# Cached values of four sequences at once, each in 32 columns of its own, in five steps between attention and output units

## What is computed

```
for g, (window, dil) in enumerate(((128, 1), (512, 4), (2048, 16))):     # 3 head groups x 4 heads of 64
    idx = L + arange(4)[:, None] - dil * arange(window // dil + 1)[None, :]
    s = einsum('bshd,bsjhd->bshj', q, ext_k[:, idx]) * 64 ** -0.5
    p = softmax(s); o = einsum('bshj,bsjhd->bshd', p, ext_v[:, idx])
o_att = sum over g of softmax_g(log-sum-exp) * o                          # then @ w_att, gates, @ w_out, FFN
```

## Time and profile before

| | |
|---|---|
| median of 3 runs | 1829.3 us |
| the profiled execution | 1829.45 us, span 1827.7 us |
| PE busy | 1750.7 us (96%), 10,208 matmul passes |
| DVE, ScalarE, GpSimd busy | 1047.1, 458.5, 74.1 us |
| granted TensorE clock, mean | 0.981 of full speed |
| share of PE in the chain that ended last | 83% |
| the 144 passes of the cached values | 899.4 to 944.8 us |

### The profile page before, as it was taken

One profiled execution on the slowest core, in us unless ns is written; L12 is line 12 of the kernel. 1 busy time (PEld: TensorE's weight loads), 2 busy tenths in 40 slices (PEclk: granted clock), 3 DMA queues, 4 the chain that ended last, 5 costly groups with the idle time before them and its releaser, 6 DMA issues.

```text
span 1827.7 us, 24930 instructions
## 1 busy us (share of the span) xinstructions
PE 1750.7 (96%) x10208; PEld 1623.5 (89%) x10208; DVE 1047.1 (57%) x1471; ACT 458.5 (25%) x900; POOL 74.1 (4%) x133
## 2 busy tenths in 40 slices
PE   5999989999998998999889999999999999999999
PEld 5899989999998888998657799899899899899897
DVE  5688998788987576586614532442433433433425
ACT  5111122323443464612202322111111111111120
POOL 0000000000000011120210000000000000000000
PEclk8999999999999999999999999999999999999999
DMA  6111243334333347984562022122222222222232
GB/s 194 52 56 58 75 134 117 104 98 165 104 111 105 136 130 223 300 278 151 190 224 75 1 81 93 63 91 89 92 92 92 92 93 92 92 92 93 92 107 100
DMA packets 156485, 211.53 MB, mean 116 GB/s; under 512 B 9090, under 2 KB 127010, under 8 KB 155603
## 3 DMA queue, kind: packets, MB, share of 16 engines
q1 hardware_dynamic: 145971, 134.01, 23.7%
q0 software_dynamic: 10416, 76.16, 11.2%
HBM read 180.04 MB, written 74.80 MB: 139 GB/s over the span
## 4 chain that ended last, share of the span: by engine, by line
PE 83%; DVE 7%; DMA 3%; DVEq 2%; SPq 1%; issue 1%; ACT 1%; ACTq 0%; POOL 0%; POOLq 0%
PE ps L723 19%; PE ps L724 19%; PE ps L725 19%; PE ps L1167 4%; PE ps L1165 4%; PE ps L1166 4%; DVE conv L1528 2%; PE ps L1091 2%; PE ps L1093 2%; PE ps L1092 2%; PE ps L937 1%; DMA qb<-scr_q 1%; SPq L489 1%; PE ps L811 1%; PE ps L990 1%
## 5 line engine op out<-in xcount | busy, mean ns | idle before, releaser
L723 PE MATMUL ps<-xhi,whi 128*128 128x352 f32 x1200 | 407.0, 339 | 8.8 <-DVEq L1584 7.3
L725 PE MATMUL ps<-xhi,wlo 128*128 128x352 f32 x1200 | 389.0, 324 | 0.0
L724 PE MATMUL ps<-xlo,whi 128*128 128x352 f32 x1200 | 388.8, 324 | 0.0
L723 PE MATMUL ps<-nhi,whi 128*128 128x352 f32 x1056 | 340.8, 323 | 0.8 <-DVE nlo L1890 0.8
L724 PE MATMUL ps<-nlo,whi 128*128 128x352 f32 x1056 | 338.5, 321 | 0.0
L725 PE MATMUL ps<-nhi,wlo 128*128 128x352 f32 x1056 | 338.2, 320 | 0.0
L1528 DVE SCALAR_TENSOR_TENSOR conv<-u,vec,conv 128x1024 f32<-128x1024 f32 x240 | 308.3, 1285 | 25.2 <-issue 10.6
L1484 DVE TENSOR_TENSOR wlo<-raw,whi 128x1024 fp32r<-128x1024 f32 x126 | 153.6, 1220 | 247.2 <-ACT whi L1255 239.0
L723 PEld LDWEIGHTS ps<-xhi,whi 128*128 128x128 f32 x1200 | 229.0, 191 | 19.6 <-DVEq L1584 7.8
L724 PEld LDWEIGHTS ps<-xlo,whi 128*128 128x128 f32 x1200 | 229.5, 191 | 4.4 <-issue 0.2
L725 PEld LDWEIGHTS ps<-xhi,wlo 128*128 128x128 f32 x1200 | 228.7, 191 | 0.0
(11 more groups left out here) (224 smaller groups left out, 2002.2 us busy)
## 6 DMA issues: line engine op xcount, KB each, us to landing
kv_sample<-cache_kv_w POOLq DMA_DIRECT2D x32, 1022.0 KB, 6.3
raw<-w_in SPq DMA_DIRECT2D x50, 512.0 KB, 4.6
raw<-w_gate_up SPq DMA_DIRECT2D x44, 512.0 KB, 3.9
scr_z<-zt SPq DMA_DIRECT2D x34, 528.0 KB, 3.2
qb<-scr_q POOLq DMA_DIRECT2D x24, 512.0 KB, 5.6
raw<-w_down SPq DMA_DIRECT2D x22, 512.0 KB, 4.2
kc<-cache_kv_w POOLq DMA_DIRECT2D x16, 512.0 KB, 6.7
vc<-cache_kv_w POOLq DMA_DIRECT2D x16, 512.0 KB, 6.0
```

The source lines that it names most:

```text
L723: pe_mm(out, wh, rhs_hi, start=first, stop=False)
L724: pe_mm(out, wh, rhs_lo, start=False, stop=False)
L725: return pe_mm(out, wl, rhs_hi, start=False, stop=last)
```

## The change

The eight sequences are taken as even ones (par 0) and odd ones (par 1). A step takes one group and one parity, four sequences x = 0..3, each with its own 32 columns of the array and its own 32 PSUM rows, and the inner loop goes over x: four matmuls in a row that share no column. Group 0 is one step with both parities. The five steps stand behind units 10 (att 10), 15 (att 15), 16, 17 and 18 (out 0, 1, 2). UNITS is shifted by one: out 0 to 3 stand before att 16. Nine buffers of a tile each are used: v5, v6, v7, v1, v2 on x1's tiles, raw0 and raw1 (the weight staging buffers), va0 and va1 (the old vc3, vc4). Group 0's tiles come four sequences per DMA. In spread_probs a semaphore stands in place of the drain. The residual tiles 1 and 2 are now loaded when steps 1 and 2 are done, 3 to 7 when step 4 is done, and the first FFN weight tile, which lay in raw0 from before att 0, is loaded after them.

```diff
-    vc = [at(f"vc{i}", [P, DEC_S, GW], F32, S3 + (KT - 3 + i) * D * 4) for i in range(3)]
-    vc += [at(f"vc{3 + i}", [P, DEC_S, GW], F32, S4 + i * D * 4) for i in range(2)]
+    v5, v6, v7, v1, v2 = (at(f"vc{t}", [P, DEC_S, GW], F32, S3 + t * D * 4) for t in (5, 6, 7, 1, 2))
+    vr = [raw[(ATT0 + i) % 2][:, :].rearrange("p (s d) -> p s d", s=DEC_S) for i in range(2)]
+    va = [at(f"va{i}", [P, DEC_S, GW], F32, S4 + i * D * 4) for i in range(2)]
+    VBUF = [[v5, v6], [v7, v1, vr[0], vr[1]], [v2, v5, v6, va[0]], [v7, vr[0], vr[1], va[1]], [v5, v6, va[0], v7]]
...
-    VTILES = [0] * 16 + [12, 12]
+    VSTEPS = [(0, 0), (1, 0), (2, 0), (1, 1), (2, 1)]
+    VSTEP_AT = {10: 0, 15: 1, 16: 2, 17: 3, 18: 4}
+    V_END = 18
...
-        for t in range(KT - 5):
+        residual_load(0)
+        att_gate_load(2)
+        for t in range(1, 3):
+            sp.wait_ge(s_kcf, t + 1)
             residual_load(t)
-        att_gate_load(2)
-        sp.wait_ge(s_pv, 1)
-        for t in range(KT - 5, KT):
+        sp.wait_ge(s_kcf, len(VSTEPS))
+        residual_load(3)
+        residual_load(4)
+        wo_load(1, 0, 2)
+        for t in range(5, KT):
             residual_load(t)
-        wo_load(1, 0, 2)
+        ffn_load(FFN0)
...
-            nc.gpsimd.memset(ptz[:, :, :, :], 0.0)
-            nc.gpsimd.memset(ptz0[:, :, :], 0.0)
+            nc.gpsimd.memset(ptz[:, :, :, :], 0.0).then_inc(s_pz, 1)
+            nc.gpsimd.memset(ptz0[:, :, :], 0.0).then_inc(s_pz, 1)
             pool.wait_ge(s_ptr, 1)
-            pool.drain()
+            pool.wait_ge(s_pz, 2)
...
-            dst = ps[32 * (b // 2):32 * (b // 2) + 32, 7, 0:GW]
-            for s in range(DEC_S if g else 1):
-                w = ptz[:, g - 1, DEC_S * b + s, :] if g else ptz0[:, b, :]
-                mm = nc.tensor.matmul(dst, w, vc[n % 5][:, s if g else DEC_S - 1, :], start=b % 2 == 0 and g == 0,
-                                      stop=b % 2 == 1 and g == NG - 1 and s == DEC_S - 1, skip_group_check=True)
+            pe.wait_ge(s_vc[n], 16 * len(VBUF[n]))
+            for s in range(DEC_S if g else 2):
+                for x in range(DEC_B // 2):
+                    if g:
+                        w, v = ptz[:, g - 1, DEC_S * (2 * x + par) + s, :], VBUF[n][x][:, s, :]
+                    else:
+                        w, v = ptz0[:, 2 * x + s, :], VBUF[0][s][:, x, :]
+                    mm = nc.tensor.matmul(ps[32 * x:32 * x + 32, 7, 0:GW], w, v, start=n == 0 and s == 0,
+                                          stop=n == len(VSTEPS) - 1 and s == DEC_S - 1, skip_group_check=True)
```

More of the change, by code:

```diff
@@ L346, in build @@
     TAP0 = KT * TAPS_GLU + 6 * NG * TAPS_QKV
[L348 to L351, removed]
-    VTILES = [0] * 16 + [12, 12]
-    V_END = len(VTILES) - 1
-    assert sum(VTILES) == NB and UNITS[V_END] == ("out", 1)
+    UNITS = [("att", c * KT + j) for c in range(2) for j in range(KT)] + [("out", t) for t in range(4)]
+    UNITS += [("att", 2 * KT + j) for j in range(4)] + [("out", 4)] + [("att", 2 * KT + j) for j in range(4, KT)]
+    UNITS += [("out", o) for o in range(5, DNG)]
+    N_EARLY = UNITS.index(("out", 5))
+    VSTEPS = [(0, 0), (1, 0), (2, 0), (1, 1), (2, 1)]
+    VSTEP_AT = {10: 0, 15: 1, 16: 2, 17: 3, 18: 4}
+    V_END = 18
+    assert UNITS[V_END] == ("out", 2)
     w_in = a["w_in"][0]
@@ L588, in _ @@
                     block_store(n)
-                if q % NCH == 1:
+                if q % NCH == 1 and GATE0 + jj + 3 < FFN0:
                     job_load(GATE0 + jj + 3)
@@ L656, in _, with value_heads, value_tile @@
             cache_copy(1, b)
+        def value_heads(par):
+            c = a[caches[0]][0, par:DEC_B:2, :, 1].rearrange("b t h d -> t b (h d)")
+            pool.dma_start(VBUF[0][par][:, :, :], c).then_inc(s_vc[0], 16)
+        def value_tile(n, x):
+            g, par = VSTEPS[n]
+            c = a[caches[g]][0, 2 * x + par, :, 1].rearrange("t h d -> t (h d)")
+            pool.dma_start(VBUF[n][x][:, :, :], c.rearrange("(i r) d -> i r d", r=DIL[g])[:, 0:DEC_S, :]).then_inc(s_vc[n], 16)
         def cache_tile(tile, sem_, kind, g, b):
@@ L695, in _ @@
         pool.wait_ge(s_g, NSLOT)
[L696 to L705, removed]
+        value_heads(0)
+        value_heads(1)
+        value_tile(1, 0)
+        value_tile(1, 1)
+        spread_probs()
+        pool.wait_ge(s_lo, ATT0 + 1)
+        value_tile(1, 2)
+        pool.wait_ge(s_lo, ATT0 + 2)
+        value_tile(1, 3)
+        value_tile(2, 0)
+        pool.wait_ge(s_kcf, 1)
+        value_tile(2, 1)
+        value_tile(2, 2)
+        pool.wait_ge(s_hlo, 2 * KT)
+        value_tile(2, 3)
+        value_tile(3, 3)
+        pool.wait_ge(s_kcf, 2)
+        for x in range(3):
+            value_tile(3, x)
+        pool.wait_ge(s_kcf, 3)
+        for x in range(3):
+            value_tile(4, x)
+        pool.wait_ge(s_kcf, 4)
+        value_tile(4, 3)
         for b in range(DEC_B):
@@ L980, in cache_values @@
         def cache_values(n):
-            g, b = n % NG, n // NG
+            g, par = VSTEPS[n]
             if n == 0:
-                pe.wait_ge(s_pz, 1)
+                pe.wait_ge(s_pz, 3)
                 pe.wait_ge(s_oTl, 5)
-            pe.wait_ge(s_vc[n % 5], 16 * (n // 5 + 1))
-            dst = ps[32 * (b // 2):32 * (b // 2) + 32, 7, 0:GW]
-            for s in range(DEC_S if g else 1):
-                w = ptz[:, g - 1, DEC_S * b + s, :] if g else ptz0[:, b, :]
-                mm = nc.tensor.matmul(dst, w, vc[n % 5][:, s if g else DEC_S - 1, :], start=b % 2 == 0 and g == 0,
-                                      stop=b % 2 == 1 and g == NG - 1 and s == DEC_S - 1, skip_group_check=True)
+            pe.wait_ge(s_vc[n], 16 * len(VBUF[n]))
[7 more added lines that the diff above has]
+                                          stop=n == len(VSTEPS) - 1 and s == DEC_S - 1, skip_group_check=True)
             mm.then_inc(s_kcf, 1)
@@ L1113, in _ @@
                 out_unit(r, i)
[L1114 to L1118, removed]
+            if r in VSTEP_AT:
+                cache_values(VSTEP_AT[r])
+            if r == V_END:
+                new_values()
             if kind == "out":
@@ L1911, in _ @@
         split_lo(1, FFN0 + 1, 0)
-        for t in range(4, NT):
+        for t in range(5, NT):
             residual(0, t)
-            if t >= 5:
-                wo_lo(1, t - 5)
+            wo_lo(1, t - 5)
         for t in range(NT + 2):
```

## The result

The changed kernel takes 1813.63 us (median of 4 runs, 1807.61 to 1814.55) against 1830.87 of the kernel before on the same chip: ratio 0.9912, 95% interval 0.9891 to 0.9932. A second set of runs gave 0.9901 (0.9885 to 0.9916). So the gain is 16 to 18 us, where 24.7 were forecast (ratio 0.987).

What follows compares the result with a forecast made beforehand. PE bounds the kernel, busy 96% of the span. The 24.7 us gain is 22.3 overlap, 1.0 step 0 now covered and 1.4 waits and clock: 1829.45 - 24.7 = 1804.8 us, range 1799 to 1814.

Steps and rivals of the forecast that it cites:

- the overlap: Value steps on PE: four column blocks run at once, 18 rounds in 8.8 us against 31.1, a gain of 22.3 us.
- the rate at which passes are handed to PE: Possible limit in the value steps: 0.061 us a pass, so 0.49 us a round rather than 0.43.
- C: Rival for the value steps: no overlap, 6.9 us a step, gain 11.2 us, 1818.2 us; chance 0.11.
- B: Rival for the value steps: two matmuls at a time, a round 0.86 us, gain 19.9 us, 1809.5 us; chance 0.14.
- what sets step 2: Ahead of step 2, PE idles from 901.0 to 907.2 for va0's load, issued only after att 15's low half is written.
- Steps 1, 3 and 4: Value steps whose tiles land in time; each should wait less than 1 us.
- The drain: GpSimd idled 9.02 us there; whether its replacement frees GpSimd earlier is swallowed by the wait ahead of step 2.
- the slow clock: Behind the wait ahead of step 2: 3 us of work at half rate, so step 2 takes 3.3 us instead of 1.96.
- the gate chunk: Load beside the value tiles: ends about 1 us later, near 887.5, inside the slack before DVE needs it at 890.06.
- the step on what is behind: Units after new_values: same work in the same dependence, residual tile 3 and the first FFN weight tile in time, nothing lost.
- part 3: Forecast's last part: the 24.7 us gained by 926.7, where out 2 is done, carries whole to the end, giving 1804.8 us.

Runs made afterwards that it cites:

- e_one_block: Changed kernel with all four sequences of a step on the first column block and first 32 PSUM rows, part of the result not computed; ratio 0.9981 to the kernel before.
- e_seq_outer: Changed kernel with the two inner loops swapped, all tokens of one sequence before the next sequence; ratio 0.9955 to the kernel before.
- e_out4_last: Changed kernel with att 16 to 23 in one piece behind out 3, so out 4 stands between att 23 and out 5; ratio 0.9894 to the kernel before.
- e_before_out4: Kernel before with out 4 moved from behind att 23 to behind out 3, so out 5 stands next to att 23; ratio 1.0041.
- e_no_release: Changed kernel with out 4 behind att 23 and buffers dealt so no step waits for the one just before it; 1800.53 us, ratio 0.9834 to the kernel before.
- e_no_release_wo: e_no_release with DVE writing each low part of the second half's output weights one out unit earlier; 1793.57 us, ratio 0.9806 to the kernel before.
- e_late_gate: Changed kernel, out 4 behind att 23, step 2's last tile in residual tile 0's place, third gate chunk loaded after step 3; ratio 0.9869 to the kernel before.
- e_drain: Changed kernel with the GpSimd drain back in place of the semaphore wait for the two memsets; ratio 0.9887 to the kernel before.
- e_v0: Changed kernel with step 2's last tile in residual tile 0's place instead of va0, residual tile 0 loaded after step 2; ratio 0.9885 to the kernel before.

## Why the prediction came out as it did

**Right: the overlap.** The prediction took full overlap of four column blocks from a glimpse of two. Measured are 1.86 us a step at full clock (1.73 would be 4 times 0.43, I took 1.96), so the rate at which passes are handed to PE is at most a small part of it. C (no overlap) is what e_one_block measures, 7.0 us a step, and the changed kernel is far from it. B fails too: a step would have taken 3.5 us.

The Trainium skill ("TensorE: Matmul & The Clock Gate", Part 3, what overlaps and what doesn't) has matmuls starting and ending in program order. The runs don't agree: a step whose passes come in pairs per block took 1.86 us, and in e_seq_outer a pass of the second sequence started at 924.54, before three of the first that precede it in the order. The same Part 3 of the Trainium skill (the mechanism, drawn for tiles in different rows) gives tiles side by side the time of one and about 4 ns for each further one. Here, for four column blocks, a round took 1.86 / 4 = 0.465 us against 0.43 for one matmul, so it is close to that but somewhat more.

**Right: what sets step 2.** PE waited 6.05 us there (6.2 forecast), for va0's load behind att 15's low half, which landed in 4.01 us (4.12 forecast). Steps 1, 3 and 4 waited for nothing. The drain made no measurable difference.

**Slightly off: the slow clock and the gate chunk.** The granted clock was 0.51 from 908.8 to 915.6, so that step 2 and the start of out 1, 5.2 us of work from 910.4 on, ran at the lower level, and not 3 us: step 2 took 3.6 us rather than 3.3, and out 1 6.4 rather than 5.75. The second gate chunk took 14.2 us to land, not some 11, and was there at 893.4, so it delayed DVE's att 8 and with it att 15's low half: the load that waits for that half was issued 27.5 us behind the first value load, against 26.9 before. Together out 3 began 930.6 - 878.9 = 51.7 us behind the first value load, where 926.7 - 876.1 = 50.6 were forecast: 1.1 us.

**Wrong: the step on what is behind.** "The rest of the list is the same work in the same dependence" was false. Out t of the first half needs chunk 2 as soon as its tokens reach beyond 704, that is from t = 5 on. Before the change out 4 stood between att 23 and out 5, and its 5.6 us covered the time in which DVE caught up with the four att units ahead of it (about 1.56 us each against PE's 0.95). The change spent that cover: with UNITS shifted by one, out 3 went ahead of att 16 and out 4 between att 19 and att 20, and nothing was left between att 23 and out 5. I counted the units and not what each may wait for. It cost 3.85 us of waiting and 18.3 - 16.7 = 1.6 of slow clock. e_out4_last takes 5.2 to 5.5 us away by undoing just this (4.7 of it in the stretch up to out 5, where 0.7 us of the wait stay), and e_before_out4 makes the wait appear in the kernel before, at 5.6 us in the same stretch. So the term of the sum that failed is part 3's, the gain at out 2 carried whole to the end: 24.7 us forecast there, of which this step lost 5.5.

24.7 less 1.1 less 5.5 is 18.1, and the remainder gained 17.8. That the measured 1813.6 us still lies in the range from 1799 to 1814 is luck: its upper part was drawn for B, which the runs refute, and no rival had a wait at out 5. Kernel and profile had all that was needed: the dependence in line 1078 and DVE's pace in the att units.

**What stays open.** Why the stage ahead of the value loads takes 870 to 880 us from one execution to the next was not tried. The changed kernel alone shows both 870.1 and 878.9; the two profiles without the change, 876.1 and 874.3, lie between. The granted clock differs too: from 700 to 870 us it was 0.94 in the changed kernel's first execution and 0.97 in its second. Nor was it tried why the same wait of 2.8 us is followed by the lower clock in some executions and not in others, and why a tile took 11.65 us to land in e_no_release.

## What to carry to other kernels

Small matmuls that use a quarter of the columns cost a quarter if four with different column blocks stand next to each other in the order; the order has to interleave them, independence is not enough. When work is moved ahead in a list, ask of the piece that it leaves behind whom it covered: the cover is lost even though all dependences are the same. Where executions differ by more than the effect, measure the stretch from an event ahead of the edit to the end, and let the ratio confirm it.

## What the runs showed of the hardware

A pass for a free column block started while three or four passes that precede it still stood in line for a busy one, but not earlier (e_seq_outer: 4.52 us for 32 passes, the time of about 20 on one block at 0.217). Waits of 3.8 and 6 us on PE were followed by some 3.4 and 6.8 us at the lower of its two clocks in the changed kernel, but in e_no_release_wo, where no wait in this stretch was longer than 1.65 us, the clock did not fall at all. Shorter waits went either way: behind 2.8 us ahead of out 9 it fell in most kernels, while in e_late_gate, with waits of 2.6 and 2.8 us, the granted clock was 1.00 from 880 to 1024. In the changed kernel the wait of 6.05 us cost about 8.5 in all: step 2 behind it was 1.8 us longer and out 1 0.65. The rows of e_late_gate and of the whole stretch in e_no_release_wo, with the granted clock of 1.00 third from the end:

```profile
880.00:1024.00 144.00, 133.85 (x749) 106.72 (x748) 74.41 (x143) 37.97 (x79) 17.43 (x27) 1.00 0.46 155
```
```profile
870.00:1024.00 154.00, 147.05 (x834) 118.37 (x833) 83.01 (x155) 43.92 (x90) 17.71 (x27) 1.00 0.43 146
```

A GpSimd drain behind value loads lasted 9.0 us in the kernel before and 10.6 in e_drain. And a load's landing time doubled, from 4.0 us in the changed kernel to 8.1 in e_v0, where the queues moved 3.69 MB from 900 to 910 us. Over 880 to 1024 us the DMA share of e_v0 is only 0.42: loads can be the bound where they meet, though they are not on the whole stretch.
